# HGRN stage of a hybrid trunk kernel: the queries' semaphore counted in three parts, the state's query placed behind the state update

## What is computed

```python
def _gla_chunked(q, k, v, logf, s0):
    # S_t = diag(f_t) S_{t-1} + k_t v_t^T, o_t = S_t^T q_t
    gc = jnp.cumsum(logf, axis=-2)
    decay = jnp.exp(jnp.where(incl, gc[..., :, None, :] - gc[..., None, :, :], -jnp.inf))
    attn = jnp.einsum('nbhid,nbhjd,nbhijd->nbhij', q, k, decay)
    q_dec = q * jnp.exp(gc)
    k_dec = k * jnp.exp(gc[..., -1:, :] - gc)
    def step(s, xs):
        o = qd_i @ s + a_i @ v_i
        s = s * gl_i[..., None] + jnp.einsum('bhcd,bhce->bhde', kd_i, v_i)
```

## Time and profile before

| | us |
|---|---|
| median of 3 runs | 1577.67 |
| lowest and highest run | 1569.42, 1578.23 |
| the profiled execution, its own time | 1578.91 |
| its span, first to last instruction | 1577.1 |
| TensorE busy in the span | 1422.9 (90%) |
| VectorE busy | 718.4 (46%) |
| from 615 to 785 us: TensorE, VectorE, GpSimd busy | 132.5, 117.9, 66.7 of 170 |
| mean granted TensorE clock, whole span, and 615 to 785 us | 0.951, 0.92 |

### The profile page before, as it was taken

One profiled execution on the slowest core, in us unless ns is written; L12 is line 12 of the kernel. 1 busy time (PEld: TensorE's weight loads), 2 busy tenths in 40 slices (PEclk: granted clock), 3 DMA queues, 4 the chain that ended last, 5 costly groups with the idle time before them and its releaser, 6 DMA issues. The chain is left out here.

```text
span 1577.1 us, 21692 instructions
## 1 busy us (share of the span) xinstructions
PE 1422.9 (90%) x8224; PEld 1059.5 (67%) x8224; DVE 718.4 (46%) x1287; ACT 407.3 (26%) x780; POOL 315.5 (20%) x450
## 2 busy tenths in 40 slices
PE   5999999999999998888698897889999999999855
PEld 1678776767898886455445545668888888888611
DVE  2656776303555563677726413533222222222246
ACT  2212121215454554122113002332212211122111
POOL 0200010102211211352443220021112111211064
PEclk9999799999999999899978898889999999999989
DMA  9645411149000001000002120159999999998687
GB/s 361 199 145 185 134 54 54 54 162 420 18 2 1 1 1 31 4 8 1 28 34 107 67 103 0 53 214 397 388 383 382 375 392 393 388 393 321 230 312 301
DMA packets 101057, 279.76 MB, mean 177 GB/s; under 512 B 22609, under 2 KB 39251, under 8 KB 99580
## 3 DMA queue, kind: packets, MB, share of 16 engines
q1 hardware_dynamic: 85148, 235.55, 40.7%
q0 software_dynamic: 15840, 43.28, 7.2%
HBM read 230.97 MB, written 64.52 MB: 187 GB/s over the span
## 5 line engine op out<-in xcount | busy, mean ns | idle before, releaser
L2601 PEld LDWEIGHTS PS<-arena 128*128 128x128 f32 x2240 | 259.9, 193 | 43.1 <-ACT arena L3085 27.6
L2601 PE MATMUL PS<-arena 128*128 128x128 f32 x2240 | 264.7, 277 | 4.8 <-DMA arena<-in_exp_w_down 3.5
L2904 DVE TENSOR_SCALAR arena<-PS,arena 128x1024 f32<-128x1024 f32 x70 | 89.9, 1284 | 142.0 <-PE PS L2609 142.0
L2609 PE MATMUL PS<-arena 128*128 128x512 f32 x280 | 137.8, 615 | 0.8 <-DVE arena L2897 0.8
L825 PE MATMUL PS<-arena 128*128 128x320 f32 x384 | 112.1, 447 | 1.5 <-DVE arena L1216 1.5
L830 PE MATMUL PS<-arena 128*128 128x320 f32 x384 | 107.3, 432 | 0.0
L2897 DVE TENSOR_TENSOR arena<-arena,PS 128x128 f32<-128x128 f32 x70 | 20.2, 288 | 183.6 <-ACT arena L3091 183.6
L3091 ACT ACTIVATE arena<-PS 128x128 f32<-128x128 f32 x70 | 19.4, 278 | 313.9 <-PE PS L2601 313.9
L825 PEld LDWEIGHTS PS<-arena 128*128 128x128 f32 x384 | 74.8, 197 | 33.4 <-issue 5.5
L830 PEld LDWEIGHTS PS<-arena 128*128 128x128 f32 x384 | 73.0, 190 | 30.4
L838 PE MATMUL PS<-arena 128*128 128x256 f32 (+1 forms) x400 | 89.4, 382 | 0.0
(11 more groups left out here) (462 smaller groups left out, 2237.9 us busy)
## 6 DMA issues: line engine op xcount, KB each, us to landing
arena<-in_exp_w_gate SPq DMA_DIRECT2D x70, 512.0 KB, 5.9
arena<-in_exp_w_up SPq DMA_DIRECT2D x70, 512.0 KB, 9.7
arena<-in_exp_w_down SPq DMA_DIRECT2D x70, 512.0 KB, 17.2
y_rows<-arena SPq DMA_DIRECT2D x70, 512.0 KB, 17.1
y_rows<-cst SPq DMA_DIRECT2D x1, 21504.0 KB, 58.3
arena<-in_w_in SPq DMA_DIRECT2D x16, 1024.0 KB, 6.2
arena<-in_w_mod SPq DMA_DIRECT2D x32, 512.0 KB, 3.7
arena<-in_w_mod SPq DMA_DIRECT2D x4, 2048.0 KB, 15.0
```

The lines of the kernel that those rows point to most:

```text
L2601: mm = pe.matmul(PS[:, bank, 0:P], w[:, k, :], xT[j % 2][:, k, :], start=k == 0, stop=k == KT - 1)
L2609: mm = pe.matmul(PS[:, 4 + 2 * (j % 2) + half, :], hid[j % 2], ed[j][:, 512 * half:512 * half + 512], start=True, stop=True)
L2904: dve.tensor_scalar(yb[j].rearrange("p (h n) -> p h n", h=2), PS[:, 4 + 2 * (j % 2):6 + 2 * (j % 2), :], gate_col[j % 2], None, ALU.mult). ...
```

## The change

`h_qe` now counts three times per unit: at the end of query part one, of part two, and at the state's query. Level 1 on TensorE waits for part one, level 4 for part two, and the unit's output for the state's query (in units 2 and later, which read it). On VectorE the state's query of unit u + 1 leaves its place ahead of the take of unit u and goes behind the state update of unit u. In unit 0, whose queries had stood in one row ahead of merge 0, that merge now comes after part one. No arithmetic is added or removed.

```diff
--- before.py
+++ after.py
@@ -1106,7 +1106,9 @@
                         pe.wait_ge(h_kTs, u + 1)
                     elif r == 1:
                         pe.wait_ge(h_ke, u + 1)
-                        pe.wait_ge(h_qe, u + 1)
+                        pe.wait_ge(h_qe, 3 * u + 1)
+                    elif r == 4:
+                        pe.wait_ge(h_qe, 3 * u + 2)
                     if (LV + 1) * u + r >= 2:
                         pe.wait_ge(h_merge, (LV + 1) * u + r - 1)
                     for pt in range(2):
@@ -1122,6 +1124,7 @@
                     pe.wait_ge(h_merge, (LV + 1) * (u + 1))
                     if u >= 2:
                         pe.wait_ge(h_staken, u - 1)
+                        pe.wait_ge(h_qe, 3 * u + 3)
                     pe.wait_ge(h_e, min(2 * u + 4, 2 * HU))
                     for pt in range(2):
                         if u >= 2:
@@ -1601,8 +1604,7 @@
                                                   halves(hE[u % 2][:, :, l, :], l)[:, :, :, half, :], ALU.mult)
                         else:
                             i = dve.tensor_tensor(hKQ[u % 2][:, :, l, :], q, hE[u % 2][:, :, l, :], ALU.mult)
-                    if LV in levels:
-                        i.then_inc(h_qe, 1)
+                    i.then_inc(h_qe, 1)
 
                 def hgrn_merge(u, r):
                     d = UNITS[u][0]
@@ -1646,8 +1648,10 @@
                 def by_column(ap):
                     return ap[:, 0:SMP].rearrange("p (r w) -> p w r", w=GW)
 
-                hgrn_queries(0, range(LV + 1))
+                hgrn_queries(0, range(3))
                 hgrn_merge(0, 0)
+                hgrn_queries(0, range(3, LV))
+                hgrn_queries(0, [LV])
                 for u in range(HU):
                     for r in range(1, LV + 1):
                         hgrn_merge(u, r)
@@ -1662,10 +1666,12 @@
                             norm_reciprocal(2, slice(4, 20))
                     if u + 1 < HU:
                         hgrn_merge(u + 1, 0)
-                        hgrn_queries(u + 1, range(3, LV + 1))
+                        hgrn_queries(u + 1, range(3, LV))
                     hgrn_take(u)
                     if u < NO_STATE:
                         hgrn_take_state(u)
+                    if u + 1 < HU:
+                        hgrn_queries(u + 1, [LV])
                     if u in (1, 4):
                         norm_means(u // 2 if u == 1 else 1)
                     elif u in (3, 6):
```

## The result

| | before | after |
|---|---|---|
| median, us | 1576.99 (4 runs) | 1555.18 (4 runs, 1552.33 to 1559.62) |
| profiled execution, its own time | 1578.91 | 1552.62 |
| span of the profile | 1577.1 | 1550.8 |

The changed kernel is faster: ratio 0.9874, 95% interval 0.9832 to 0.9916. The forecast was 1562.7 in a range of 1556 to 1571, with 0.36 for a gain above 1%. The median fell by 21.8 us and the profiled time by 26.3.

The account below looks back on a forecast made before the run. In the HGRN stage VectorE and TensorE wait for each other, level 1 for `h_qe`. Unit gains of 18.4 us less 3.4 for low clock give 15.0, so a median of 1562.7 from 1577.67; range 1556 to 1571.

Parts of the forecast that it names:

- What holds level 1: HGRN units: level 1 reads the first of eight queries but waits for the last; "issue" waits, 35.5 us, are for `h_qe`.
- Level 3 as the later of two chains: HGRN units: level 3 starts at the later of keys ready plus 0.1 plus 2 x 1.70 and merge 1 plus 0.80.
- the signs: Changed profile, HGRN stage: expected marks, among them level 3 starting 0.8 us after merge 1's start in all units.
- The held units: Units 1, 4 and 8, query held by a long GpSimd instruction: gains 4.6, 3.9 and 4.6, together 13.1 us.
- The gross sum: All HGRN units before costs: 3.4 + 13.1 + 1.1 + 0.8 = 18.4 us.
- about 30: VectorE in the HGRN stage: the merges' waits were to fall from 39.6 us to about 30.
- The clock: TensorE, levels 3 to 5: low clock after gaps ahead of level 3 costs 3.4 us, between nothing and 5.1.
- the clock holds: Rival, HGRN stage: no low stretch follows TensorE's shorter gaps, all 18.4 us kept, 1559.3; chance 0.20.
- The barrier behind the stage passes a gain on.: End of the HGRN stage: the gain there reaches the kernel's time, 15.0 us.
- The chances: Whole kernel: 0.36 for faster by over 1%, 0.62 for within 1%, 0.02 for slower by over 1%; forecast case 0.48.
- Slower: Rival, HGRN units: query ahead of merge 1 is held by GpSimd in every unit, 5.9 us slower, 1583.6; chance 0.04.
- the rule of two SBUF inputs: State's query on VectorE: reading two SBUF inputs contends with GpSimd wherever placed; by that alone the move saves nothing.

Follow-up runs that it names:

- the four pieces: Kernel before, with GpSimd's two 128x1280 squares cut into four of 128x320 each; one profiled execution, stage 163.2 us, 3.2 less than before.
- the count alone: Changed kernel with the three-part semaphore kept but the state's query back ahead of the take; 1558.38 us, ratio 0.9886.
- the shifted kernels: Changed kernel with 10 or 25 dummy VectorE multiplications ahead of unit 0; behind the stage 790.3 and 778.6 us.
- the second of the changed kernel: Changed kernel profiled again, no edit; median 1557.14 us, ratio 0.9885, stage 148.6, behind the stage 779.0.
- the second trace of the kernel before: Kernel before, profiled once more without an edit; behind the stage 784.1 us, where its first trace had 787.9.
- the one shifted by 6 us: Changed kernel with ten dummy VectorE multiplications ahead of unit 0; behind the stage 790.3 us.
- the one shifted by 19 us: Changed kernel with 25 dummy VectorE multiplications ahead of unit 0; median 1571.63 us, ratio 0.9988.

## Why the prediction was right, and where not

- **What holds level 1.** Right. The "issue" waits were waits for `h_qe`; level 1 now starts 0.05 us after its keys in units 1 to 7 and 9, and 0.4 after in unit 8.
- **Level 3 as the later of two chains.** Right, and the best supported step: eight of nine units came out within 0.35 us of their term, and in units 1 to 9 level 3 starts 0.78 to 0.80 behind merge 1, as the signs had it. The later level 1 cost only where TensorE's chain ends last, and an earlier merge 1 paid only where VectorE's does.
- **The held units.** Right in size, 13.3 measured against 13.1. That the count gives about 9 of this and the move 4.4 was tested apart. The hold by a GpSimd instruction, and its end with that instruction, is shown by the four pieces.
- **The gross sum.** 18.0 for units 1 to 8 against 17.6 predicted (the 18.4 less unit 9's 0.8). The prediction did not say that this sum leaves out every low stretch of the kernel before, some 6.6 us of it by the estimate above; it counted the low clock as a cost to come, and named what was there in units 1 and 8 only in passing. The merges' waits fell further than the "about 30" of its signs, to 23.5.
- **The clock.** This is the term that was mis-sized: 3.4 us, "two such stretches, as unit 2 is the row nearest to it". Unit 2's gap of 2.4 us brought no low stretch in the changed kernel (1.00 over the levels behind it), though one of that kind did in the kernel before and with the count alone. Only unit 8's came, and cost 1.46 (level 3 to level 4 took 3.16 in place of 1.70), in both traces of this kernel. Without it unit 9's -0.5 would be 0.9. The stage's gain was thus 17.8, and the rival "the clock holds" (18.4) was nearer than the forecast. That it was one stretch and not two is partly luck: in the shifted kernels the same order had one behind unit 2 as well, or a double one behind unit 8, and units 2 to 9 took 1.0 and 1.5 us longer.
- **"The barrier behind the stage passes a gain on."** It did, and more: 10.0 us fell off behind it in the first traces, 8.9 in the second of the changed kernel; against the second trace of the kernel before it is 6.2 and 5.1. The prediction had only 2 to 3 us for the spread of the runs. This step failed in size. The runs showed the code behind the stage take 777.9 to 790.3 us under shifts alone. The median's gain beyond the stage was 4.0 us in the first set and 1.6 in the second (19.4 less 17.8). A steady part cannot be told from the spread here.
- **The chances.** 0.62 for a change within 1% was too much, and the clock term is enough to explain it: the stage's 17.8 us alone would have been 1.13%.
- **Slower, and the rule of two SBUF inputs** (the Trainium skill, "GPSIMD Engine Reference", "Specifications"). The query is held at its new place too: 1.02 in units 1 and 4, 1.19 in unit 2 and 1.59 in unit 8, where GpSimd had a long instruction, and each time it ends some 0.28 us behind that instruction. It took 0.41 to 0.43 in the other five. The take and the state update, with one operand in PSUM, took 0.41 and 1.15 beside the same GpSimd instructions (unit 8: 740.88 and 741.21, L2084 from 740.68 to 743.70). The traces agree with the rule. The rival fell since five of nine units had no hold, and in the others most of it was over by then.

## What to carry to other kernels

A semaphore that is counted once at the end of a group makes the first reader wait for the last writer; count it where the first reader's part ends. Read what such a split can give from the next place where both engines meet, not from the wait that it removes: TensorE was idle 1.37, 1.37 and 5.33 us ahead of level 1 in units 7, 5 and 8, and the gains were 1.0, 0.0 and 4.6. And look at what the granted clock does behind a wait: here, by the estimate above, over a third of what the shorter waits gave came from low stretches that no longer followed them. And move work that an engine must do out of the stretch in which it is the late one, into a gap in which it waits: that beat the change itself by 5 us in the stage.

## What the runs showed of the hardware that was not expected

- The same gap of TensorE, at the same place in the same order of instructions, was followed by the low clock in one kernel and not in another: 2.41 us ahead of level 3 of unit 2 in the changed kernel (1.00 behind it), 2.40 us in the one shifted by 19 us (0.50 from 681.7).
- Behind the stage, the low clock that begins with the barrier's gap lasted 23.9 us in the kernel before (787.7 to 811.6), 13.7 in the changed one (771.9 to 785.6) and 23.9 in the one shifted by 6 us, with the same program behind it. It ran on while TensorE was busy: 19.73 of the 20 us from 791 to 811 in the trace of before, at 0.50.
- The same kernel under the profiler twice gave its low stretches at the same places within 0.1 us (the changed kernel), or not quite so: in the second trace of the kernel before most come about 3 us earlier, like the stage itself, but the one at 664.8 is twice as long, from 658.6, and the two of 3.4 us at 43.6 and 1466.9 did not come.
